# Mixer 1 reordered: head norms before the scans, recurrence sums a panel later, the root by logarithm

## What is computed

```python
u = conv(lru_x)                                   # causal, width 4, 512 channels
r, i = sigmoid(u @ w_r + b_r), sigmoid(u @ w_i + b_i)
log_a = -8 * r * softplus(-lam)
h = scan(a=exp(log_a), b=sqrt(-expm1(2 * log_a)) * (i * u))     # h_t = a_t h_(t-1) + b_t
y_lru = h * gelu(lru_g)
y_sb  = stick_breaking_attention(sb_q, sb_k, sb_v)
y_fox = softmax attention of rms(fx_q) * g, rms(fx_k) * g with a forget bias
y = concat(rms(y_lru), rms(y_sb), rms(y_fox)) * g_mix_out
out = y @ w_out
```

## Time and profile before

| | us |
|---|---|
| median of 3 runs | 1614.84 |
| lowest and highest | 1614.66, 1617.54 |
| profiled execution, its time | 1614.81 |
| profiled execution, its span | 1613.0 |

### The profile page before, as it was taken

The page is one execution under the profiler, slowest core; times in us unless marked ns, Lnnn a source line. Parts: engine busy times, 40 slices in busy tenths (PEclk is TensorE's granted clock), DMA queues, the critical chain, the costliest instruction groups (busy, mean ns, idle before and its releaser), DMA issues.

```text
span 1613.0 us, 32436 instructions
## 1 busy us (share of the span) xinstructions
PE 1570.0 (97%) x13288; PEld 1549.7 (96%) x13288; DVE 1285.8 (80%) x1935; ACT 912.1 (57%) x1569; POOL 237.5 (15%) x255
## 2 busy tenths in 40 slices
PE   4999999999999999999999999999999999999998
PEld 3999998999999999998999999999999999999998
DVE  6688888788788888888688898788888878786553
ACT  5445458664555545458665445666645466664453
POOL 4122000022210122000022231001222010021100
PEclk9999999999999999999999999999999999999999
DMA  9899974559988799874459988534899873457761
GB/s 346 330 305 323 317 266 137 183 169 329 314 311 314 265 317 314 310 244 150 165 187 344 317 309 289 181 105 157 292 330 336 309 251 130 132 182 239 239 215 42
DMA packets 110996, 403.11 MB, mean 250 GB/s; under 512 B 12562, under 2 KB 12818, under 8 KB 110720
## 3 DMA queue, kind: packets, MB, share of 16 engines
q1 hardware_dynamic: 109280, 395.87, 71.2%
q0 software_dynamic: 1568, 5.17, 1.2%
HBM read 399.94 MB, written 1.05 MB: 249 GB/s over the span
## 4 chain that ended last, share of the span: by engine, by line
PE 86%; DVE 8%; ACT 3%; DMA 1%; issue 1%; SPq 0%; DVEq 0%; ACTq 0%
PE PS L552 85%; DVE WL L1690 2%; DVE SCR L1693 1%; DMA ring<-in_ada 1%; DVE SCR L1690 1%; ACT WH L1205 1%; DVE ring L1716 1%; DVE SCR L2049 0%; DVE SCR L1687 0%; DVE SMALL L2087 0%; ACT SCR L1495 0%; DVE SMALL L2048 0%; PE PS L1041 0%; DVE MOD L1687 0%; ACT HH L1237 0%
## 5 line engine op out<-in xcount | busy, mean ns | idle before, releaser
L1690 DVE TENSOR_TENSOR WL<-ring,WH 128x1024 fp32r<-128x1024 f32 (+1 forms) x508 | 604.2, 1224 | 191.3 <-ACT WH L1205 190.4
L552 PE MATMUL PS<-HH,WH 128*128 128x256 f32 (+1 forms) x2640 | 632.3, 281 | 3.3 <-ACT WH L1205 3.3
L552 PE MATMUL PS<-HL,WH 128*128 128x256 f32 (+1 forms) x2640 | 618.4, 278 | 0.0
L1205 ACT ACTIVATE WH<-ring 128x1024 fp32r<-128x1024 f32 (+1 forms) x508 | 511.4, 1049 | 47.6 <-PE PS L552 45.9
L552 PEld LDWEIGHTS PS<-HH,WH 128*128 128x128 f32 x2640 | 497.6, 189 | 4.4 <-ACT WH L1205 3.4
L552 PEld LDWEIGHTS PS<-HL,WH 128*128 128x128 f32 x2640 | 492.9, 189 | 0.6
L552 PE MATMUL PS<-HH,WL 128*128 128x256 f32 (+1 forms) x2640 | 378.0, 279 | 2.5 <-DVE WL L1690 2.3
L552 PEld LDWEIGHTS PS<-HH,WL 128*128 128x128 f32 x2640 | 338.7, 189 | 3.7 <-DVE WL L1690 3.7
L1716 DVE CUSTOM_DVE_ANT_0 ring<-ring,CB,VC 128x1024 f32<-128x1024 f32 x238 | 330.7, 1407 | 11.5 <-DMA ring<-in_ada 11.4
L552 PE MATMUL PS<-AH,WL 128*128 128x256 f32 x1056 | 293.0, 277 | 1.1 <-DVE WL L1690 1.1
L552 PE MATMUL PS<-AH,WH 128*128 128x256 f32 x1056 | 293.2, 278 | 0.0
(11 more groups left out here) (214 smaller groups left out, 1480.7 us busy)
## 6 DMA issues: line engine op xcount, KB each, us to landing
ring<-in_up SPq DMA_DIRECT2D x176, 512.0 KB, 5.6
ring<-in_ada SPq DMA_DIRECT2D x144, 512.0 KB, 6.0
ring<-in_ffn SPq DMA_DIRECT2D x132, 512.0 KB, 4.8
ring<-in_mod SPq DMA_DIRECT2D x96, 512.0 KB, 5.8
ring<-in_down SPq DMA_DIRECT2D x88, 512.0 KB, 5.6
ring<-in_win SPq DMA_DIRECT2D x64, 512.0 KB, 5.4
ring<-in_wout SPq DMA_DIRECT2D x32, 512.0 KB, 4.7
ring<-in_winv SPq DMA_DIRECT2D x8, 512.0 KB, 4.5
```

Of the source, the lines that this page charges most:

```text
L552: return e.matmul(out, lhsT, rhs, start=start, stop=stop, skip_group_check=skip)
L1205: e.activation(half_of(i)[0], slot_of(("half", i, 0))[:, 0:w], ACT.Copy).then_inc(s_hi, 1)
L1690: return e.tensor_tensor(out, a, b, op)
```

## The change

- POOL takes gelu's last product, GT = GT * LG, 128x1024 (`s_gelu`), which DVE did.
- The root on ACT is made as Ln (with a tiny bias) and Exp, in place of Sqrt. Two table loads go: the one that Sqrt needs and the `lnexp()` behind it. ACT now does the squares for the head norms ahead of the root.
- DVE does `lo(u0 + 7)`, `head_norms`, `lo(u0 + 8)`, both `maxima` and the halves of `lo(u0 + 9)` before the four scans.
- `recurrence_sums` moves from panel 8 to panel 9, behind `stick_scores(1)`. The square and the inverse root on ACT move with it; `hi(u0 + 9)` moves ahead of `spread`. The wait for `s_gnr` moves from `fox_turn` to `fox_values`, and the sums wait for `by_keys(1)`.
- One ada panel goes from the first mixer to the feed-forward block before it. Each mixer 1 now has four ada halves, loaded behind halves 21, 21, 21 and 23, and reduced later.

```diff
-ADA_N = (21, 3, 19, 19, 2, 19, 2, 21, 2, 4)
+ADA_N = (22, 2, 19, 19, 2, 19, 2, 21, 2, 4)
-SHARE_AT = {"mix1": (17, 17, 19, 19, 21, 23), ...}
+SHARE_AT = {"mix1": (21, 21, 21, 23), ...}
@@ POOL
+                    e.wait_ge(s_lrut, l + 1)
+                    e.tensor_tensor(GT, GT, LG, ALU.mult).then_inc(s_gelu, 1)
@@ TensorE
-                        if r == 1:
-                            e.wait_ge(s_gnr, l + 1)
 ...
                 def fox_values():
+                    e.wait_ge(s_gnr, l + 1)
 ...
                 def recurrence_sums():
+                    e.wait_ge(s_apt, r0 + 2)
 ...
                     stick_scores(1)
+                    recurrence_sums()
                     stick_sums(0)
 ...
                     stick_scores(0)
-                    recurrence_sums()
@@ ACT
-                e.wait_ge(s_om, l + 1)
-                e.activation(TT, TT, ACT.Sqrt).then_inc(s_mult, 1)
                 projected(5, FXR[:, 2:4, :], 1)
                 e.activation(sq, FXR, ACT.Square).then_inc(s_fxsq, 1)
+                e.wait_ge(s_om, l + 1)
+                step(e.activation(TT, TT, ACT.Ln, bias=tiny, scale=1.0))
+                e.activation(TT, TT, ACT.Exp, scale=0.5).then_inc(s_mult, 1)
                 hi(u0 + 7)
-                lnexp()
 ...
                 hi(u0 + 8)
-                e.wait_ge(s_ylru, l + 1)
-                e.activation(GT, LG, ACT.Square).then_inc(s_gnsq, 1)
+                hi(u0 + 9)
                 spread(SBK, 1).then_inc(s_proj, 1)
-                hi(u0 + 9)
                 exponents(0)
                 exponents(1)
                 stick_logs(0)
+                by_keys(0)
+                projected(8, FXV, 0)
+                e.wait_ge(s_ylru, l + 1)
+                e.activation(GT, LG, ACT.Square).then_inc(s_gnsq, 1)
+                hi(u0 + 10)
+                by_keys(1)
                 e.wait_ge(s_gnss, l + 1)
                 (Ln, Exp -> s_gnr)
-                by_keys(0)
-                projected(8, FXV, 0)
-                hi(u0 + 10)
-                by_keys(1)
                 by_keys(2)
@@ DVE
-                e.wait_ge(s_lrut, l + 1)
-                tt(GT, GT, LG, ALU.mult)
 ...
+                lo(u0 + 7)
+                head_norms()
+                lo(u0 + 8)
+                maxima(0)
+                lo_half(2 * u0 + 18)
+                maxima(1)
+                lo_half(2 * u0 + 19)
                 (root times input, four scans)
-                lo(u0 + 7)
+                e.wait_ge(s_gelu, l + 1)
                 tt(LG, U, GT, ALU.mult).then_inc(s_ylru, 1)
-                head_norms()
-                lo(u0 + 8)
-                share(n, 0), share(n, 1), maxima(0), maxima(1), lo(u0 + 9), share(n, 2), share(n, 3)
+                stick_softplus(0)
+                lo(u0 + 10)
                 (four products with the root -> s_gny)
-                stick_softplus(0)
-                lo(u0 + 10)
+                share(n, 0), share(n, 1)
                 stick_softplus(1)
 ...
-                share(n, 4)
-                lo(u0 + 11)
+                share(n, 2)
                 diagonal(n, o0)
                 diagonal(n, o0 + 1)
+                lo(u0 + 11)
```

More of the change, by code:

```diff
@@ L70 @@
 OUT0 = {1: 0, 4: 4, 6: 8, 8: 16}
-SHARE_AT = {"mix1": (17, 17, 19, 19, 21, 23), "mix2": (21, 22, 23, 23)}
+SHARE_AT = {"mix1": (21, 21, 21, 23), "mix2": (21, 22, 23, 23)}
 def half_panel(n, q):
@@ L158, in build @@
         s_gny, s_gnh, s_gnl = sem("s_gny"), sem("s_gnh"), sem("s_gnl")
-        s_u, s_gate, s_gelusq, s_gelup, s_sig, s_lrut, s_lrue = (sem("s_" + k) for k in (
-            "u", "gate", "gelusq", "gelup", "sig", "lrut", "lrue"))
+        s_u, s_gate, s_gelusq, s_gelup, s_gelu, s_sig, s_lrut, s_lrue = (sem("s_" + k) for k in (
+            "u", "gate", "gelusq", "gelup", "gelu", "sig", "lrut", "lrue"))
         s_om, s_mult, s_ylru = sem("s_om"), sem("s_mult"), sem("s_ylru")
@@ L325, in build @@
         rs0, rs1 = SM_[:, 0:2], SM_[:, 2:4]
+        tiny = SM_[:, 8:9]
         def first_rank(i):
@@ L490, in ts @@
                     return e.tensor_scalar(out, a, c1, c2, op0) if op1 is None else e.tensor_scalar(out, a, c1, c2, op0, op1)
+                e.memset(tiny, 2.0 ** -120)
                 e.wait_ge(s_lamr, 1)
@@ L1986, in mixer1 @@
                     stt(LG[:, k, :], LG[:, k, :], vec(f"gmix{l}", k), GT[:, 0, :], ALU.mult, ALU.mult).then_inc(s_gny, 1)
-                stick_softplus(0)
-                lo(u0 + 10)
+                share(n, 0)
+                share(n, 1)
                 stick_softplus(1)
@@ L2003, in mixer1 @@
                 partial(n, 1)
-                share(n, 5)
+                share(n, 3)
                 partial(n, 2)
```

## The result

| | before | after |
|---|---|---|
| median us (4 runs each) | 1614.75 | 1599.64 |
| lowest to highest | 1610.52 to 1617.54 | 1598.92 to 1605.81 |
| profiled execution, its time | 1614.81 | 1599.55 |
| its span | 1613.0 | 1597.5 |

What follows compares the result with a forecast made beforehand. TensorE, busy 97% of the span, bounds the kernel. Per mixer 4.3 - 0.4 for POOL - 0.1 for small waits gives 3.8, 7.6 for two: 1614.81 becomes 1607.2 us, range 1604.9 to 1611.5.

Steps and rivals of the forecast that it cites:

- the moved panel: First feed-forward block: two more ada halves, up to 3.3 us if the ring falls behind; taken as nothing, TensorE not waiting.
- A: The main forecast: 1605.8 to 1608.8 us, with POOL's price 0.1 to 0.75 and two slacks about held; chance 0.58.
- The mixers: Both mixers 1: 3.8 us won in each, 7.6 in all.
- five waits: TensorE in each mixer 1: squares 0.47, lo(u0 + 7) 0.91, head_norms 1.30, exponents(0) 0.85, diagonal 0.46; 4.8 us with lost overlap.
- new stall before chunk 2: Each mixer 1: TensorE waits 0.5 us for stick_weights(1) on ACT, leaving 4.3 us won of 4.8.
- POOL's lock: Gelu's product on POOL blocks DVE's two-input instruction, making TensorE late by 0.1 to 0.75 us per mixer; 0.4 taken.
- the 0.1 for small waits: Each mixer: 0.1 us deducted for small waits at places with slack under 1 us.
- B: POOL's product costs TensorE nothing, chunk 2's stall is smaller: 4.3 to 4.8 us per mixer, 1605.2 to 1606.2; chance 0.12.
- C: Stalls return in the mixer's second half: gain 2.3 to 2.7 us per mixer, 1609.4 to 1610.2, or 1612; chance 0.17.
- D: The mixers' gain is given back in the feed-forward blocks, where DMA sets the pace: 1613 to 1615 us; chance 0.08.
- E: Slower: the later recurrence chain holds up by_keys(1) and the sums; at 6 us of delay 1617.4 us; chance 0.05.
- its chain: Recurrence chain in each mixer 1: the root's product was forecast to start 48.1 us behind the mixer's first point.

Runs made afterwards that it cites:

- e2: Kernel before with only the ada panel moved from the first mixer to the feed-forward block ahead of it; ratio 0.9994 to the kernel before.
- e1: The changed kernel again, no edit; runs at 1600.79 to 1603.04 us (7) and 1605.89 to 1609.26 (5), ratio 0.9959 to the kernel before.
- e3: Changed kernel with the ada panel left in the first mixer and two more shares behind share 3; ratio 0.9969 to the kernel before.
- e11: e10 with DVE's root product and four scans again ahead of lo(u0 + 7); 1606.76 us.
- e12: e10 with Sqrt and its two table loads again on ACT, Sqrt ahead of projected(5); 1605.94 us.
- e9: Kernel before plus e6's eight narrow-weight matmuls in block 0 ahead of tick 3; median 1610.46 us.
- e5: e4 plus 14 TensorE matmuls before block 0; runs at 1597.02 to 1597.65 us (4) and 1604.73 to 1606.76 (3).
- e6: e4 plus 8 matmuls with 4-column weights in block 0 ahead of tick 3; 1599.03 to 1602.12 us.
- e10: Changed kernel plus e6's eight narrow-weight matmuls in block 0 ahead of tick 3; median 1600.77 us.
- e13: e5 plus 2 narrow-weight matmuls in block 0 and 2 behind the stop at 931 us; 1597.52 to 1599.44 us, ratio 0.992 to the kernel before.
- e14: e5 plus 8 narrow-weight matmuls in block 0 alone; 1598.16 to 1599.89 us, ratio 0.9925 to the kernel before.
- e8: e4 plus 8 float32 matmuls with 128x128 weights in block 0 ahead of tick 3; 1608.15 to 1611.28 us.
- e7: e4 plus one TensorE wait in block 0 ahead of tick 4, for ACT's silu of tick 3; 1600.23 to 1603.34 us.
- e4: Changed kernel with gelu's last product back on DVE; ratio 0.9946 to the kernel before.

## Why the prediction was wrong, point by point

**What failed.** The step that failed is the one on the moved panel and the first block: "TensorE does not wait there", and so "I take nothing", with which the sum went from "The profiled execution took 1614.81" straight to 1607.2. Both halves of it hold for the panel (e2: 0.9994), but the sum took it for granted that matmuls without a wait take the same time in every execution. They don't: block 0 has about 1700 matmuls at 117.8 or 113.3 ns, 7 us apart. The median that I started from, 1614.84 from three runs, was of executions at the slow pace, the less frequent one (29 of 98). I subtracted the mixers' gain from that, and four new executions of after fell mostly on the other side. Half of the 15.1 us is this draw, 7.1 us in the two traces. No run shows a part of the change in it (e1, e2, e3). Had both medians been of one pace, the difference would have been near 8.4 and the median after near 1606.4, within A; that the first three runs were all slow was bad luck, for which the range had no room.

**What was right.** The mixers: 7.6 forecast, 8.4 to 8.5 in the traces. All five waits went. The squares (no wait; a forecast of 270.85 to start right behind panel 6 holds), `lo(u0 + 7)`, the head norms, `exponents(0)` and `diagonal` no longer show. The new stall before chunk 2 is 0.26 where 0.5 was forecast. POOL's lock is real and cost 0.27 against 0.4; the 0.1 for small waits was not needed. These three make 0.24, 0.13 and 0.1 us; each mixer gave 0.4 to 0.5 more than the forecast 3.8.

**The rivals.** B would have been near for the mixers alone: 4.2 to 4.3 lies at its edge. C did not come: the trace shows no wait for `by_keys(1)` or `stick_softplus(1)`. D did not: nothing was given back in the feed-forward blocks. E did not: its chain kept to the forecast times (48.17 for 48.1) and held up nothing. None of the rivals, nor the range, had a place for a pace that changes between executions.

**What the profile had shown.** In the trace of before, block 0 starts 342 matmuls in 40 us, and a later block 356 in 40, both at a clock of 1.00 and without a pause:

```profile
350.00:390.00 40.00, 40.00 (x356) 40.00 (x355) 34.20 (x47) 24.18 (x36) 8.99 (x8) 1.00 0.83 292
```

A comparison of these counts would have raised the question beforehand. The three runs would not: all were in the slow cluster, 0.18% apart.

**What is left.** In the mixer of the changed kernel TensorE goes at 117.8 ns from the head sums at 266 us to 293 us, with no wait and no narrow weights between. 143 of its weight matmuls start there; at 4.5 ns each, 113.3 ns would win an estimated 0.6 us in each mixer. No run tries it.

## What to carry to other kernels

Where TensorE is busy without a wait, count its matmuls per microsecond in each block; here two blocks of like work with different counts were worth more than all the waits of a mixer. Before a median of three runs is taken as the base of a sum, ask whether the runs could be of two kinds, and compare stretches between points that both traces have, not whole spans. A wait removed in a mixer is priced well from the timeline, step by step; each moved operation should also be asked what it now stands in front of (the two shares of e3). A wait can cost more than its length: look at the granted clock behind it (e11).

## What the runs showed of the hardware

- TensorE has two paces for 128x256 fp32r matmuls with 128 new weight columns each, at a granted clock of 1.00 (2.4 GHz): 113.3 and 117.8 ns from start to start. It kept one for some 185 us in block 0 of before (slow); in e12's mixers it turned from slow to fast with no wait or other weights between. Which one block 0 gets differs between executions of the same program (29 of 98 slow before, 5 of 12 in e1). With TensorE's clock down at the start both paces came (before, e9), and the slow one with the clock up (e5).
- Matmuls with 4-column weights set it to fast: no time of e6, e9, e10, e13 and e14 is in the slow cluster, of 36, and the traces of e6, e10, e13 and e14 show the switch. A float32 group with 128 columns set it to slow in block 0 (e8, 10 of 10 by their times), but not for long in e12's mixers. A stop set it to fast in e7 and drew it anew near 931 us (4 of 16 traces slow). Why the stream has two paces is not shown.
- Without the pause ahead of block 0, the clock did not fall at all (1.00 from 36 to 40 us in e5); e5's fastest execution is 0.8 us under e4's, which ran in another set. Behind a stop of 1.89 us in e11 it fell to 0.50 for 3.41 us, in both mixers, and matmuls of 256 columns started 213 ns apart.
- A float32 product of 128x1024 on POOL takes some 2.35 us (3.13 from its issue), and a DVE instruction with two SBUF inputs beside it took 2.12 us in place of 0.41.
